# The routing between the last mixer and the first expert: ranks by shifted bfloat16 products, another order of lists, rows and scatters

## What is computed

```python
def moe_swiglu(h, w_router, w_gate_e, w_up_e, w_down_e):
    logits = (xt @ w_router).astype(jnp.float32)
    top_val, top_idx = lax.top_k(logits, TOP_K)
    gates = jax.nn.softmax(top_val, axis=-1)
    flat_e = top_idx.reshape(-1)
    order = jnp.argsort(flat_e)
    tok = order // TOP_K
    sizes = jnp.bincount(flat_e, length=N_EXPERTS).astype(jnp.int32)
    xs = xt[tok]
    hg = lax.ragged_dot(xs, w_gate_e, sizes)
    hu = lax.ragged_dot(xs, w_up_e, sizes)
    ys = lax.ragged_dot(jax.nn.silu(hg) * hu, w_down_e, sizes)
    ys = ys * gates.reshape(-1)[order][:, None].astype(ys.dtype)
    out = jnp.zeros_like(xt).at[tok].add(ys)
```

## Time and profile before

| what | value |
|---|---|
| runs shown, median (lowest to highest) | 3603.13 us (3601.9 to 3603.52) |
| the profiled execution's own time | 3602.58 us |
| its span, first to last instruction | 3600.8 us |
| PE busy | 3513.5 us, 98% of the span |
| DVE, ACT, POOL busy | 1803.4, 1540.2 and 203.1 us |
| mean granted TensorE clock | 0.991 of full speed |
| traffic | 540.81 MB, mean 150 GB/s |

### The profile page before, as it was taken

One profiled execution on the slowest core, in us unless ns is written; L12 is line 12 of the kernel. 1 busy time (PEld: TensorE's weight loads), 2 busy tenths in 40 slices (PEclk: granted clock), 3 DMA queues, 4 the chain that ended last, 5 costly groups with the idle time before them and its releaser, 6 DMA issues. The chain is left out here.

```text
span 3600.8 us, 71968 instructions
## 1 busy us (share of the span) xinstructions
PE 3513.5 (98%) x27356; PEld 3343.2 (93%) x27356; DVE 1803.4 (50%) x2599; ACT 1540.2 (43%) x2207; POOL 203.1 (6%) x207
## 2 busy tenths in 40 slices
PE   8999899999999999979999999999999999999997
PEld 7888799999999989879899898998999999999997
DVE  5455553333333454365565565555655544545544
ACT  3455433333333333354454544544545434434433
POOL 1000000000000000040010010100101000100100
PEclk9999999999999999989999999999999999999999
DMA  5111323223332322256575565655655545554543
GB/s 192 36 51 39 135 94 99 93 94 122 96 98 94 123 94 84 94 195 210 185 237 193 192 230 186 232 195 194 228 192 198 188 156 180 190 167 154 184 160 124
DMA packets 158043, 540.81 MB, mean 150 GB/s; under 512 B 23480, under 2 KB 23520, under 8 KB 157920
## 3 DMA queue, kind: packets, MB, share of 16 engines
q1 hardware_dynamic: 129440, 467.72, 39.4%
q0 software_dynamic: 23872, 62.99, 5.0%
q10 hardware_dynamic: 4608, 8.39, 0.6%
HBM read 515.54 MB, written 45.48 MB: 156 GB/s over the span
## 5 line engine op out<-in xcount | busy, mean ns | idle before, releaser
L302 DVE TENSOR_TENSOR wl<-wraw,wh 128x1024 fp32r<-128x1024 f32 x884 | 1082.6, 1225 | 1309.2 <-ACT wh L298 1290.2
L298 ACT ACTIVATE wh<-wraw 128x1024 fp32r<-128x1024 f32 x884 | 934.5, 1058 | 1138.1 <-PE ps L316 1130.5
L316 PE MATMUL ps<-exh,wh 128*128 128x240 f32 (+3 forms) x3588 | 1017.9, 284 | 4.8 <-issue 4.8
L316 PE MATMUL ps<-exh,wl 128*128 128x240 f32 (+3 forms) x3584 | 1017.4, 284 | 3.4 <-issue 3.2
L316 PE MATMUL ps<-exl,wh 128*128 128x240 f32 (+3 forms) x3584 | 1017.5, 284 | 0.4 <-issue 0.4
L316 PE MATMUL ps<-xs,wh 128*128 128x256 f32 x5248 | 820.8, 279 | 2.4 <-DVE qAl L746 2.0
L316 PEld LDWEIGHTS ps<-xs,wh 128*128 128x128 f32 x5248 | 698.2, 189 | 12.5 <-issue 8.5
L316 PEld LDWEIGHTS ps<-exh,wh 128*128 128x128 f32 x3588 | 676.3, 189 | 5.7 <-issue 5.3
L316 PEld LDWEIGHTS ps<-exh,wl 128*128 128x128 f32 x3584 | 675.7, 189 | 3.8 <-issue 3.8
L316 PEld LDWEIGHTS ps<-exl,wh 128*128 128x128 f32 x3584 | 675.9, 189 | 1.7 <-issue 1.5
L316 PE MATMUL ps<-xs,wl 128*128 128x256 f32 x2624 | 513.8, 277 | 0.0
(11 more groups left out here) (318 smaller groups left out, 3511.2 us busy)
## 6 DMA issues: line engine op xcount, KB each, us to landing
wraw<-in_w_expert SPq DMA_DIRECT2D x676, 512.0 KB
wraw<-in_w_main SPq DMA_DIRECT2D x208, 512.0 KB
hT<-in_xT POOLq DMA_DIRECT2D x2, 2048.0 KB, 10.4
h_d<-hT POOLq DMA_DIRECT2D x2, 2048.0 KB, 10.0
hT<-h_d POOLq DMA_DIRECT2D x2, 2048.0 KB, 13.8
xrow_d<-rows ACTq DMA_DIRECT2D x16, 256.0 KB, 2.0
hrow_d<-rows ACTq DMA_DIRECT2D x16, 256.0 KB, 3.1
yraw<-y_d POOLq DMA_DIRECT2D x4, 768.0 KB, 7.8
```

What stands on the lines that cost most here:

```text
L298: act.activation(wh[:, j], wraw[:, j], ACT.Copy).then_inc(hi_done, 1)
L302: dve.tensor_tensor(wl[:, j], wraw[:, j], wh[:, j].bitcast(F32), ALU.subtract).then_inc(lo_done, 1)
L316: mm = pe.matmul(out[:, s], a, b[:, s], start=first and part == 0 and c == 0, stop=last and part == 2 and d == n)
```

## The change

Ranks and counts come from nine bfloat16 products of the one-hot sums (`sentb`), each shifted by one token tile, instead of three float32 products on running sums. `route_dve` computes the first list ahead of the bases and the table; the slots and the gates move to a new `slots_dve`, behind DVE's part of `turn_x`. The table counts by slots / CAP over NIT = 13 items in place of a pairwise comparison of 24 candidates. ACT issues the store of one `xrow_d` half row after it has started the copy of the next; the last eight `hrow_d` stores move from ACT to POOL, one after each of the first eight units of the first item, and `rows` moves so that it can be read that long. The exponential of the gates, two of the first four `hi_part` and three of the first four `lo_part` move behind `turn_x`. The list scatters wait until PE has used 16 units of the first item. One `logits_pe` of the second half goes one unit earlier, the list product stands two rows later in PE's order, and the squares of the norm beside an item go two to three units later.

```diff
+NIT = NE + 2 * T // CAP
-SLOTS = (NCAND + 1) * CAP
+SLOTS = (NIT + 1) * CAP
...
-                if u >= 2:
-                    logits_pe(pe, 1, u - 2)
+                if u >= 1:
+                    logits_pe(pe, 1, u - 1)
...
-            for k in (6, 7):
-                logits_pe(pe, 1, k)
+            logits_pe(pe, 1, KD - 1)
...
                 if e == 5:
-                    pe.wait_ge(sent_ok, 1)
-                    pe.wait_ge(t_root, 2)
-                    pe.matmul(bank(SMALL, NT * NE, RANK), below[:], sent[:].rearrange("p t e -> p (t e)"), start=True, stop=False)
-                    pe.matmul(bank(SMALL, NT * NE, RANK), ones[:], before[:, 0:NT].rearrange("p t e -> p (t e)"), start=False, stop=True)
-                    pe.matmul(bank(SMALL, NE, COUNT), ones[:], before[:, NT], start=True, stop=True).then_inc(rk_mm, 1)
+                    ranks_pe(pe)
             for e in range(8):
-                if e == 4:
+                if e == 6:
                     list_pe(pe)
...
+        def ranks_pe(pe):
+
+            pe.wait_ge(sent_ok, 1)
+            pe.wait_ge(t_root, 2)
+            n = (NT + 1) * NE
+            pe.matmul(bank(SMALL, n, RANK), belowb[:], sentb[:], start=True, stop=False)
+            for back in range(1, NT + 1):
+                m = n - back * NE
+                mm = pe.matmul(bank(SMALL, m, RANK + back * NE), onesb[:], sentb[:, 0:m], start=False, stop=back == NT)
+            mm.then_inc(rk_mm, 1)
...
+        def last_rows_pool(pool):
+
+            pool.wait_ge(row_cp, 32)
+            for e in range(8):
+                t, b = 4 + e // 2, e % 2
+                pool.wait_ge(unit_used, 4 * Q_MOE + e + 1)
+                pool.dma_start(hrow_d[t * P:t * P + P, 512 * b:512 * b + 512], rows[:, e]).then_inc(last_st, 16)
+            for b in range(ROWS):
+                pool.wait_ge(row_st[b], 48)
+            pool.wait_ge(last_st, 16 * 8)
+            pool.sem_inc(rows_out, 1)
...
             for e in range(8):
-                row_act(act, 16 + e, 8 + e, 4 + e // 2, e % 2, True, XB[e])
-            act.wait_ge(gap_ok, 1)
-            act.activation(gt[:, 1], gt[:, 0], ACT.Exp).then_inc(g_exp, 1)
-            for e in range(8):
-                row_act(act, 24 + e, 16 + e, 4 + e // 2, e % 2, False, HB[e])
-                if e >= 4:
-                    hi_part(act, Q_MOE, e - 4)
+                row_copy_act(act, 16 + e, 8 + e, 4 + e // 2, e % 2, True, XB[e])
+                if e >= 1:
+                    row_send_act(act, 15 + e, 4 + (e - 1) // 2, (e - 1) % 2, True)
+            row_send_act(act, 23, 7, 1, True)
+            for e in range(8):
+                row_copy_act(act, 24 + e, 16 + e, 4 + e // 2, e % 2, False, HB[e])
+            for j in range(2):
+                hi_part(act, Q_MOE, j)
...
+                if u == KD + 3:
+                    dve.wait_ge(r_cst, 9)
+                    dve.tensor_copy(belowb[:], below[:])
+                    dve.tensor_copy(onesb[:], ones[:])
+                    dve.memset(sentb[:, NT * NE:], 0.0)
+                    dve.tensor_copy(tokb[:].rearrange("p t a -> p (t a)"), tokf[:].rearrange("p t a -> p (t a)"))
...
+            dve.tensor_tensor(sentb[:, 0:NT * NE], pick[:, 0].rearrange("p t e -> p (t e)"), pick[:, 1].rearrange("p t e -> p (t e)"),
+                              ALU.add).then_inc(sent_ok, 1)
             dve.tensor_tensor(sent[:], pick[:, 0], pick[:, 1], ALU.add)
-            own(dve.memset(before[:, 0], 0.0))
-            for t in range(NT):
-                last = dve.tensor_tensor(before[:, t + 1], before[:, t], sent[:, t], ALU.add)
...
-            own(dve.tensor_copy(count, bank(SMALL, NE, COUNT)))
...
             dve.max_index(least[:], best8[:], late[:, 1]).then_inc(first_ok, 1)
-            own(dve.tensor_tensor(smaller, over_f(key), over_e(key), ALU.is_lt))
+            dve.scalar_tensor_tensor(val[:], rank, 1.0, sent[:], ALU.add, ALU.mult)
+            own(dve.tensor_scalar(only, late[:, 1], best8[:, 0:1], None, ALU.is_equal))
+            own(dve.tensor_tensor(placed[:, 1], val[:], over_t(only), ALU.mult))
+            own(dve.tensor_reduce(lowest[:], placed[:, 1], AX.X, ALU.add))
+            for t in range(NT):
+                dve.tensor_scalar(mine[:, t], range_c[:], lowest[:, t:t + 1], None, ALU.is_equal).then_inc(mine_ok, 1)
+            dve.wait_ge(list_mm, 1)
+            own(dve.tensor_scalar(firstf[:].rearrange("p s a -> p (s a)"), bank(LOGIT1, 2 * CAP // P, LIST), float(NT), None, ALU.add))
+            dve.scalar_tensor_tensor(tokl0[:], firstf[:, :, 0], float(P), firstf[:, :, 1], ALU.mult, ALU.add).then_inc(list_ok, 1)
...
             pool.memset(ybuf[:], 0.0).then_inc(y_z, 1)
+            pool.memset(hg[:], 0.0).then_inc(hg_z, 1)
+            pool.memset(xg[:], 0.0).then_inc(hg_z, 1)
+            pool.wait_ge(hg_z, 2)
+            for half, g in ((0, fga), (1, fgb)):
+                pool.dma_start(g[:], io["final_norm"][512 * half:512 * half + 512].partition_broadcast(P)).then_inc(f_in, 16)
+            last_rows_pool(pool)
             pool.wait_ge(slots_ok, 1)
             pool.wait_ge(gates_ok, 2)
+            pool.wait_ge(unit_used, 4 * Q_MOE + 16)
             for t in range(NT):
...
+                if i == 2 and r == 3:
+                    dve.wait_ge(rows_out, 1)
...
@@ def _(act):
-            act.wait_ge(items_ok, 1)
-            n_items = act.value_load(nitem[0:1, 0:1], min_val=1, max_val=NCAND)
             act.sem_inc(on_free, 2)
             turn_x_act(act, 0, XB0)
+            for j in (2, 3):
+                hi_part(act, Q_MOE, j)
+            gap_exp_act(act)
+            act.wait_ge(items_ok, 1)
             act.wait_ge(y_z, 1)
-            for b in range(ROWS):
-                act.wait_ge(row_st[b], 16 * (32 // ROWS))

             by_width(act, lambda it, n: item_act(act, it, n))
+            n_items = act.value_load(nitem[0:1, 0:1], min_val=1, max_val=NIT)
...
@@ def _(dve):
+            lo_part(dve, Q_MOE, 0)
             turn_x_dve(dve, 0, XB0)
+            for j in range(1, 4):
+                lo_part(dve, Q_MOE, j)
+            slots_dve(dve, own)
+            dve.wait_ge(items_ok, 1)
             dve.wait_ge(y_z, 1)
```

More of the change, by code:

```diff
@@ L185, in build @@
         sent = sb("sent", [P, NT, NE], F32, s4)
+        sentb = sb("sentb", [P, (NT + 1) * NE], BF16, s4)
+        belowb, onesb = (sb(n, [P, P], BF16, s4) for n in ("belowb", "onesb"))
+        val = sb("val", [P, NT, NE], F32, s4)
         place0 = sb("place0", [P, 8, NE], F32, s4)
-        before = sb("before", [P, NT + 1, NE], F32, s4)
         place = sb("place", [P, NT, NE], F32, s4)
@@ L213, in build @@
         s4 = ExitStack()
-        sb("under_mine", [P, 2 * KD * T + ROWS * 512], F32, s4)
+        sb("under_rows", [P, 2 * KD * T + KD * T // 2], F32, s4)
+        rows = sb("rows", [P, ROWS, 512], F32, s4)
+        s4.close()
+        s4 = ExitStack()
+        sb("under_mine", [P, 2 * KD * T], F32, s4)
         rw = sb("rw", [P, KD, NE], F32, s4)
@@ L1621, in route_dve @@
             dve.wait_ge(rk_mm, 1)
-            count, more, rest, key, base_r, base_f, shift, room = (place0[:, v] for v in range(8))
+            more, rest, nkey, only, base_r, base_f, shift, room = (place0[:, v] for v in range(8))
             smaller = placed[:, 0]
+            count = bank(SMALL, NE, COUNT)
+            rank = bank(SMALL, NT * NE, RANK).rearrange("p (t e) -> p t e", e=NE)
             def over_e(v):
@@ L1700, in route_dve, with slots_dve, over_t @@
             dve.tensor_copy(upto[:], uptof[:])
-            own(dve.tensor_tensor(eq[:], icnt[:].rearrange("p (i a) -> p i a", a=1).to_broadcast([1, NCAND + 1, NCAND]),
-                                  cand[:, 5:6].to_broadcast([1, NCAND + 1, NCAND]), ALU.is_equal))
-            own(dve.tensor_tensor(pk[:], eq[:], cand[:, 3:4].to_broadcast([1, NCAND + 1, NCAND]), ALU.mult))
+            own(dve.tensor_tensor(eq[:], icnt[:].rearrange("p (i a) -> p i a", a=1).to_broadcast([1, NIT + 1, NCAND]),
+                                  cand[:, 5:6].to_broadcast([1, NIT + 1, NCAND]), ALU.is_equal))
+            own(dve.tensor_tensor(pk[:], eq[:], cand[:, 3:4].to_broadcast([1, NIT + 1, NCAND]), ALU.mult))
             own(dve.tensor_reduce(itf[:], pk[:], AX.X, ALU.add))
             dve.tensor_copy(itab[:], itf[:]).then_inc(items_ok, 1)
-            for j in range(4):
-                lo_part(dve, Q_MOE, j)
+        def slots_dve(dve, own):
+            more, rest, nkey, only, base_r, base_f, shift, room = (place0[:, v] for v in range(8))
+            def over_t(v):
+                return v.rearrange("p (a e) -> p a e", a=1).to_broadcast([P, NT, NE])
+            own(dve.tensor_tensor(shift, base_f, base_r, ALU.subtract))
+            own(dve.tensor_tensor(shift, shift, rest, ALU.subtract))
+            own(dve.tensor_tensor(place[:], val[:], over_t(rest), ALU.is_gt))
+            own(dve.tensor_tensor(place[:], place[:], over_t(shift), ALU.mult))
```

(19 more changed lines are left out.)

113 lines of the change are left out of this document (37 added, 76 removed).

## The result

The changed kernel took a median of 3662.39 us (3650.95 to 3663.73, 4 runs), the kernel before 3603.32 us (3601.9 to 3608.07, 4 runs) beside it: ratio 1.0151, 95% interval 1.0139 to 1.0163. The forecast was 3581. The profiled execution took 3663.73 us, its span is 3661.7 us, 60.9 more than before. Granted clock 0.993 (0.991 before), traffic 540.78 MB (540.81). So neither the clock nor more data explains it.

What follows compares the result with a forecast made beforehand. PE, busy 98% of the span, was taken as the bound, leaving its idle or slow places. Terms -8.9 - 14.1 + 0.9 + 0.4 = -21.7 on 3602.6 gave 3580.9, said as 3581 us; range 3576 to 3594.5.

Steps and rivals of the forecast that it cites:

- rival D: Beside the first item's weight traffic, half the moved scatters take 4.81 us each, starving PE: loses 42 us, 3626; chance 0.04.
- Rival C: During the moved scatters PE runs at slow-stretch pace, losing 17.6 us plus a 2.7 us half-speed wake: 3601; chance 0.05.
- Logits +0.4: Logits one unit earlier delay the last unit's end and its dependents: +0.4 us, bounds 0 and +0.9.
- Ranks -0.9, first expert -1.4, list -6.1: In the routing, DVE starts 0.9 us earlier, the first expert's index comes 1.4 earlier and the first list 6.1 earlier.
- Rows and gather: start -8.9: Earlier row stores, gather at 1544.5 and rows 2.2 us after its issue: first item starts at 1555.45, 8.9 us earlier.
- the early end: Earliest gather start, 1544.3, the list plus 1 us; the late end, 1547.9, follows the last row store; forecast took 1544.5.
- rival B: Row stores still land 7.3 us after issue, the gather 5.2 after its own: start only -2.5, total 3587; chance 0.13.
- Slow stretch -14.1, +0.9 back: At the first item's entry, moving the scatters away saves 14.1 us; 0.9 us is kept back for cold code.
- Rival A, cold code: The stall belongs to entering a loop and stays without scatters; only the start moves: 3594; chance 0.12.
- Behind the turn 0: Work of ACT and DVE moved behind the turn into the first item costs nothing, with cover of 2 to 3 us.
- Table, POOL's new order, DVE's wait for `rows_out`: 0: Table done before its first need, covered by 1.4 us; POOL's reordered work and DVE's wait behind its 12th unit cost nothing.
- End +0.4: ACT loads `nitem` after the last item, ahead of the last root: 0.29 us plus handling, +0.4 us.

Runs made afterwards that it cites:

- a_pad: The changed kernel with `spare` enlarged, so the buffers behind the small tables regain their old addresses, 64 bytes higher: 3587.55 us, ratio 0.9968 to the kernel before.
- b_m64: The kernel before with only `spare` made 16 words smaller, so the buffers behind it stand 64 bytes lower: 3660.81 us.
- b_w256: The kernel before with 256 bytes of small tables moved ahead of the weights, which stand 256 bytes higher while `xs` stays: 3607.06 us.
- a_held: `a_pad` with SP's first weight loads of the expert held until all row stores have landed: 3587.84 us.
- b_scat16: The kernel before with POOL's clears and gains load first and the 16 list scatters behind 16 units of the first item: 3595.59 us, ratio 0.9973.
- a_tail: `a_pad` with the loads of `nitem` on ACT and DVE put back ahead of the items: 3588.66 us.
- a_early: `a_pad` with the list scatters ahead of the last row stores and without the wait for 16 units: 3594.93 us.

## Why the prediction was wrong

**The step that failed is one that isn't there.** The part-by-part costing takes each instruction that is removed, added or moved, and gives the smaller table a price only on DVE (25 entries to 14). That it moves the buffers behind it by 64 bytes has no term, and no rival. The sum, both ends of the range and the 0.04 for slower all take it for granted that stages without an edit keep their time. In those stages it cost 50.2 + 16.7 + 2.7 - 2.2 = 67.4 us, more than the whole difference of 60.9. `a_pad` shows it in one direction and `b_m64` in the other, with 65.1 us in the same four stretches and no edit at all; the edits themselves gave the rest back. Only rival D lay on the slower side, and not for this reason: the holes beside the scatters that C and D speak of cost 5.9 us in the profile.

With placement made equal, `a_pad` against before, the steps can be read one by one.

- *Whole.* 0.9968, 11.5 us faster; forecast 22 on the profiled execution (there: 15.4 of span). 3588 lies inside the range of the forecast, on the side that it gave, but at half its gain: the two large terms below were both too big, and the scatters' one was right for a wrong reason.
- *Logits +0.4.* PE waited 0.35 us for `acc` behind its last logits step. The squares came 2.1 us after the last unit's addition instead of 2.6, while that addition itself stands behind one more step (0.9 us). Together +0.4 or +0.5: right in size, not separated by a run. What is counted below from the last addition leaves these 0.9 us out.
- *Ranks -0.9, first expert -1.4, list -6.1.* Index -2.7, list -7.3 in the changed kernel. The nine bfloat16 products took about 0.4 us where I took 0.7. Right, a little cautious.
- *Rows and gather: start -8.9.* It was -4.3 (34.6 to 30.3 us). The old routing took 34.6 to 36.1 us here in seven profiles (42.0 in `b_w256`), the new one 29.6 to 30.3 in five and 34.1 in the changed kernel itself, where the gather waited longest; why it did is open. Mis-sized in two terms. The gather was to start 1.2 us after the list, near the early end, "since the weights no longer overlap the last stores much": it starts 4.8 after it, and 1.7 where the weights are held back (`a_held`). And the rows were to land 2.2 us after the last issue, because the `hrow_d` stores have left: they take 4.9. Taking those stores away saved nothing here; whose traffic the 4.9 us are wasn't separated. This is rival B in part, and its sign came up, a gather released by a row store later than 1546: 1549.5 in the changed kernel (past the late end of 1547.9), 1546.7 in `a_pad`, both counted from the last addition.
- *Slow stretch -14.1, +0.9 back.* First item 245.7 to 233.9, -11.8. Its mechanism ("scatters don't slow running code; they delay its fetch") was wrong: `b_scat16` and the changed kernel lose 6 us beside the scatters in code that has long run. Rival C named the place, at 0.05, with a loss of 20 us. And 14.1 was a high draw: in seven other programs with the old routing the first item is 6.5 (`b_m64`) to 12.4 us (`b_w256`) over the next. Moving the scatters alone brought 0.27% (`b_scat16`; the medians differ by 7.0 us), with 6.5 us lost at their new place in the profile.
- *Rival A, cold code.* Out: without scatters at the entry the first item of `a_tail` is 2.0 us over the others and of `a_held` 0.9, and PE waits for nothing at "issue" from 1550 to 1640. The Trainium skill ("Runtime: NRT & Kernel Launch", Instruction fetch mechanics) says that a taken branch to code not already held has to wait for its fetch. In these profiles no such wait of PE shows at the entry.
- *Behind the turn 0.* In `a_pad` 2.4 us: ACT waited 1.5 and 1.2 us for weights of the next turn. A small miss.
- *Table, POOL's new order, DVE's wait for `rows_out`: 0.* Right in the changed kernel; `a_early` shows the last one's price when its cover goes.
- *End +0.4.* It was +2.1 (`a_pad`), of which the load's place explains 0.3 to 0.9. The nine profiles of the old routing have 19.7 to 20.8 us there, so the 19.7 of before is their low end.
- *Sums.* Three were written down wrong, without a share in the miss. C's loss comes to 17.2 us from its own numbers, not 17.6. D passes the time of before at 22 us of loss, but the verdict "slower", 7.2 us further, only at 29. And the terms of the table as given end at about 1547, not 1549.3; it was done at 1548.2.

With PE alone, the same 48 float32 products take 5.56 to 5.87 us, by the distance of the two operands. The Trainium skill ("TensorE: Matmul & The Clock Gate", Step-by-step: what each phase is for) says that PE has two independent read ports into SBUF, so that loading the next weights takes nothing from the running product. I had costed a moved buffer at nothing, as if the place of the two operands never mattered to these two reads, without saying so. For these products it does matter; whether it is the two reads that meet, no run shows.

## What to carry to other kernels

When a diff changes the size of any on-chip buffer, write down which buffers move against which, and give that a term: compare the count of products per 100 us in a stretch that the diff does not touch before reading anything else. Busy time and clock don't show it. If the count differs, pad back to the old distance first, and only then judge the edit. A loss beside a burst of indirect DMAs may come up again where the burst is moved to, and it differs from one profile to the next, so read several executions before giving its removal a price.

## What was new of the hardware

- The pace of float32 products of width 256 (declared float32r in these kernels) depends on the distance between weight tile and streamed operand, with a period of 256 bytes: 5.56 us per 48 at 192, 5.72 to 5.87 at the other steps of 32, but for a second sweep in which 64 took 5.56 as well. A whole kernel of 3600 us gets 44 to 63 us slower by it.
- Beside sixteen indirect stores of 128 x 8 bytes, about 22 us long, PE lost between 0 and 14 us, much of it with "remote" waits of ACT and DVE that end with the last of them. Why, and why not always, stays open.
- A gather of 0.96 MB in rows of 4 KB (three indirect DMAs) needed 3.9 to 5.5 us from the end of its last issue to its first reader in twelve profiles, with or without 2 MB of other stores in the way, 6.3 us in `b_w256`, and 7.6 us both in `a_held`, where weight loads started just behind it, and in `b_scat16`.
